# All four granules of the last two pairs split instead of two split and two in fp32

## What is computed

```
mod = jax.nn.silu(c) @ w_mod + b_mod
shift, scale, gate = jnp.split(mod, 3, axis=-1)
h = rms_norm(x, g_pre) * (1.0 + scale[:, None, :]) + shift[:, None, :]
proj = h @ w_in
```

## Time and profile before

| | us |
|---|---|
| median of 3 runs (2849.79 to 2851.85) | 2849.89 |
| the profiled execution's own time | 2849.23 |
| its span | 2847.5 |

### The profile page before, as it was taken

How to read it: one execution, slowest core, us unless ns; L and a number is a source line. 1 busy time by engine, 2 the same in 40 slices (tenths; PEclk the granted TensorE clock), 3 DMA queues, 4 the chain that set the end, 5 groups by cost and what they waited for, 6 DMA issues and landing times.

```text
span 2847.5 us, 35784 instructions
## 1 busy us (share of the span) xinstructions
PE 2803.5 (98%) x13342; PEld 2302.4 (81%) x13342; DVE 1767.3 (62%) x2180; ACT 1382.0 (49%) x1879; POOL 36.2 (1%) x69
## 2 busy tenths in 40 slices
PE   8899999999999999999999999999999999999998
PEld 5588887888887888888888888788888888888886
DVE  7789899777656556554544556675555545445565
ACT  3355646456544454544554544445444445545443
POOL 0000000000000000000000000000000000000000
PEclk8999999999999999999999999999999999999999
DMA  9987798865655555565555566555555655555664
GB/s 398 409 306 236 280 344 306 287 221 179 206 177 183 170 171 178 175 222 192 171 178 177 174 196 223 178 178 170 173 177 190 206 192 170 178 177 176 196 213 148
DMA packets 159991, 603.73 MB, mean 212 GB/s; under 512 B 18376, under 2 KB 18576, under 8 KB 154464
## 3 DMA queue, kind: packets, MB, share of 16 engines
q1 hardware_dynamic: 155376, 583.08, 59.8%
q0 software_dynamic: 4464, 18.55, 2.0%
HBM read 599.41 MB, written 2.14 MB: 211 GB/s over the span
## 4 chain that ended last, share of the span: by engine, by line
PE 93%; DVE 3%; DMA 3%; ACT 1%; issue 0%; SPq 0%; ACTq 0%; DVEq 0%
PE acc L785 63%; PE acc L2334 19%; DMA raw<-in_w 3%; PE psT L733 2%; PE psS L766 1%; PE psS L756 1%; PE psS L2334 1%; PE psT L2247 1%; PE psS L2300 1%; PE psT L2260 1%; PE psT L739 1%; PE psS L2319 0%; PE psT L2225 0%; DVE wlo L1771 0%; PE psS L2272 0%; PE psS L773 0%
## 5 line engine op out<-in xcount | busy, mean ns | idle before, releaser
L434 DVE TENSOR_TENSOR wlo<-raw,whi 128x1024 fp32r<-128x1024 f32 x670 | 820.3, 1225 | 868.0 <-ACT whi L322 866.6
L322 ACT ACTIVATE whi<-raw 128x1024 fp32r<-128x1024 f32 x670 | 709.2, 1059 | 996.0 <-PE acc L785 974.9
L785 PE MATMUL acc<-whi,tokens_hi 128*128 128x512 f32 x2304 | 637.4, 398 | 3.5 <-DVE tokens_lo L279 1.9
L785 PE MATMUL acc<-whi,tokens_lo 128*128 128x512 f32 x2304 | 619.1, 390 | 0.0
L785 PE MATMUL acc<-wlo,tokens_hi 128*128 128x512 f32 x2304 | 618.9, 390 | 0.0
L785 PEld LDWEIGHTS acc<-whi,tokens_lo 128*128 128x128 f32 x2304 | 432.8, 188 | 92.2
L785 PEld LDWEIGHTS acc<-wlo,tokens_hi 128*128 128x128 f32 x2304 | 432.8, 188 | 91.5
L785 PEld LDWEIGHTS acc<-whi,tokens_hi 128*128 128x128 f32 x2304 | 422.5, 188 | 84.0 <-DVE tokens_lo L440 2.2
L1771 DVE TENSOR_TENSOR wlo<-raw,whi 128x1024 fp32r<-128x1024 f32 x160 | 195.4, 1223 | 99.3 <-ACT whi L1468 98.8
L1468 ACT ACTIVATE whi<-raw 128x1024 fp32r<-128x1024 f32 x160 | 168.7, 1058 | 181.4 <-PE acc L2334 117.0
L2334 PE MATMUL acc<-whi,tokens_hi 128*128 128x512 f32 x800 | 225.5, 402 | 1.9 <-DVE tokens_lo L1870 1.2
(11 more groups left out here) (353 smaller groups left out, 2268.8 us busy)
## 6 DMA issues: line engine op xcount, KB each, us to landing
raw<-in_w SPq DMA_DIRECT2D x838, 512.0 KB, 3.4
raw<-in_w_late SPq DMA_DIRECT2D x80, 512.0 KB, 5.0
mraw<-in_w SPq DMA_DIRECT2D x64, 512.0 KB, 4.7
mraw<-in_w_late SPq DMA_DIRECT2D x48, 512.0 KB, 4.8
y<-in_w_early SPq DMA_DIRECT2D x12, 1024.0 KB, 14.2
mraw<-in_w_early SPq DMA_DIRECT2D x7, 1024.0 KB, 13.8
scr<-in_w_early SPq DMA_DIRECT2D x7, 1024.0 KB, 13.5
sgl<-in_w_early SPq DMA_DIRECT2D x6, 1024.0 KB, 14.6
```

Of the source, the lines that this page charges most:

```text
L322: act.activation(whi[:, n % SLOTS, :], raw[:, n % SLOTS, :], ACT.Copy).then_inc(s_hi, 1)
L434: dve.tensor_tensor(wlo[:, n % SLOTS, :], raw[:, n % SLOTS, :], whi[:, n % SLOTS, :].bitcast(F32), ALU.subtract).then_inc(s_lo, 1)
L785: m = pe.matmul(acc[c % 2][:, tb, :], a[:, kk, tb * P:(tb + 1) * P], b[:, n % SLOTS, k * CW:(k + 1) * CW], start=(kk == 0 and q == 0), sto ...
```

## The change

`direct` now holds for granules below `R_SPLIT` (24) instead of 32. So in pairs 6 and 7 the granules 24, 25, 28 and 29 are split as well. They use slots 0 and 1 of `raw`, `whi` and `wlo`; the transfer of granule 28 waits for the `lo` of 24 and that of 29 for the `lo` of 25, and those of granule 32 and of the first `w_late` tile wait for the `lo` of 28 and 29. ACT gets four `hi` more, DVE four `lo`, PE 48 split matmuls for 16 in fp32. ACT's `fill_hi` of pairs 6 and 7 is moved from the first step of the pair to its third. PE's first granule of these pairs waits for `tokens_lo` instead of `zt`.

```diff
--- before.py
+++ after.py
@@ -959,7 +959,7 @@
 
 def direct(n):
 
-    return n < R_RING and n % TOGETHER[0] < DIRECT
+    return n < R_SPLIT and n % TOGETHER[0] < DIRECT
 
 
 def splits(n):
@@ -970,6 +970,21 @@
 def landing(n):
 
     return divmod(DIRECT * (n // TOGETHER[0]) + n % TOGETHER[0], LANDINGS)
+
+
+def place_of(n):
+
+    return landing(n)[1] if direct(n) else n % SLOTS
+
+
+def turns_before(i, n):
+
+    return sum(not direct(m) for m in range(i, n, SLOTS))
+
+
+def last_in(i, n):
+
+    return max(m for m in range(n) if place_of(m) == i)
 
 
 def done(l, c):
@@ -984,6 +999,7 @@
 R_RING = TOGETHER[0] * GPC
 DIRECT = 2
 LANDINGS = 3 * DIRECT
+R_SPLIT = TOGETHER[0] * (GPC - 2)
 R_FULL = (63, 64, 70, 99, 100, 107, 115, 119)
 RING = SLOTS + 2
 CLOSE1 = 2
@@ -1038,8 +1054,8 @@
 
 
     if item in ITEM:
-        return ITEM[item] // RING + 1 + (R_RING // SLOTS if DIRECT <= ITEM[item] % RING < SLOTS else 0)
-    return item[1] // SLOTS + 1
+        return ITEM[item] // RING + 1 + (turns_before(ITEM[item] % RING, R_RING) if ITEM[item] % RING < SLOTS else 0)
+    return turns_before(item[1] % SLOTS, item[1] + 1)
 
 
 def h_fill(l, r):
@@ -1376,7 +1392,7 @@
                 sp.dma_start(whole(n), dram["w1"][n]).then_inc(s_d[landing(n)[1]], 16)
                 return
             if n >= SLOTS:
-                sp.wait_ge(*split(n - SLOTS))
+                sp.wait_ge(*released(last_in(n % SLOTS, n)))
             sp.dma_start(slot(("w", n)), dram["w1"][n]).then_inc(s_w[n % SLOTS], 16)
 
         def item(k):
@@ -1385,7 +1401,7 @@
             if k >= RING:
                 sp.wait_ge(*consumed(ITEMS[k - RING]))
             elif k < SLOTS:
-                sp.wait_ge(*released(max(n for n in range(R_RING) if (landing(n)[1] if direct(n) else n % SLOTS) == k)))
+                sp.wait_ge(*released(last_in(k, R_RING)))
             else:
                 sp.wait_ge(s_macc, EARLY - (EARLY - 1) % len(big))
             src = dram["w1"][i] if kind == "w" else dram["w_late"][i]
@@ -1589,7 +1605,7 @@
                     fill_hi(("h", l, h_fill(l, r)))
                 if r == GRAN1 - 1:
                     act.activation(one[:], eps[:, 0:1], ACT.Sqrt)
-                if l == 0 and r in range(TOGETHER[0], R_RING, TOGETHER[0]):
+                if l == 0 and r in list(range(TOGETHER[0], R_SPLIT, TOGETHER[0])) + list(range(R_SPLIT + 2, R_RING, TOGETHER[0])):
                     fill_hi(("h", l, r // TOGETHER[0]))
                 if not direct(GRAN1 * l + r) and (l == 0 or r >= AHEAD):
                     hi(GRAN1 * l + r)
@@ -2406,9 +2422,9 @@
                 continue
             c, g = place(l, r)
             if l == 0 and r < R_RING:
-                if c == 0:
+                if direct(r) and c == 0:
                     pe.wait_ge(s_aff, g + 1)
-                if c == DIRECT:
+                if c == (DIRECT if direct(r - c) else 0):
                     pe.wait_ge(s_h, g + 1)
             elif c == 0:
                 pe.wait_ge(s_h, GPC * l + g + 1)
```

## The result

| | before | changed |
|---|---|---|
| median, us | 2850.52 (2849.78 to 2851.91, 6 runs) | 2873.89 (2870.49 to 2875.87, 6 runs) |
| ratio to before | | 1.0083 [1.0073, 1.0092] |
| span of the profiled execution | 2847.5 | 2868.8 |

What follows compares the result with a forecast made beforehand. It took transfers to bound the opening and PE, without gaps, the long rest. Terms +2.0 (tile 29), +1.3 (tokens_lo), -1.6 (fp32 matmuls gone), +0.8 (hole) make +2.5, forecast 2852.4 us, range 2849.4 to 2857.0.

Steps and rivals of the forecast that it cites:

- The early pairs: Pairs ahead of pair 6: claimed untouched by the change, with no term in the sum.
- Pair 6 on ACT and DVE: Later tokens_hi and a third lo start DVE's tile 29 at 126.2 to 126.5 instead of 124.16; taken as +2.0.
- The hand-over and PE in pair 7: PE starts pair 7 on tokens_lo instead of zt, +1.3; four split granules take 10.9 instead of 12.44, -1.6.
- The clock in pair 6: PE, idle 7.3 before pair 6, then runs slow and loses 1.7; bounds 0 to +0.9 on pair 7's start, taken 0.
- the cover: Room for a slow clock: PE ends pair 6 at 133.7 at full clock, and its next start is 135.8.
- The hole: Wait at 147.84 before the small product, behind the emptied queue and ACT's hi of granule 35: longer by +0.8.
- my upper bound: Latest landing of granule 35's transfer, 149.5, with the small product then starting at 151.8, +3.2.
- my +1.8 at granule 32: PE starts granule 32 at 146.7 instead of 144.96, after its four split granules of pair 7.
- (a): Rival: DVE absorbs the added lo, so the fp32 saving shows; -0.2, or -3.1 if pair 6 counts too; chance 0.12.
- (b): Rival: PE's clock stays low through all of pair 6, pair 7 starts 8.8 later; +10.6, 2860.5; chance 0.08.
- (c): Rival: emptied queue costs more, granule 32's or 35's transfer later than the bound; with 3 more 2855.9; chance 0.12.

Runs made afterwards that it cites:

- e1_places: Changed kernel with place_of giving a direct granule a slot number only where it lands in raw; 2856.34 us, ratio 1.0023.
- e2_waits: Kernel before with only the transfers of granules 6, 7, 18 and 19 waiting for the matmuls of 4, 5, 16 and 17; 2868.25 us, ratio 1.0063.
- e3_first: Kernel before with only the transfers of granules 6 and 7 waiting for the matmuls of 4 and 5; 2859.71 us, ratio 1.0031.
- e6_pair7: e1_places with R_SPLIT at 28, so only pair 7 has four split granules; 2853.13 us, ratio 1.001.
- e5_copies: e1_places with ACT's copies of chunks 2 and 3 moved right behind the hi of granule 33; 2850.92 us, ratio 1.0002.
- e7_pair7_copies: e6_pair7 with the copies of chunks 2 and 3 moved as in e5_copies; 2850.19 us, ratio 1.0.
- e4_second: Kernel before with only the transfers of granules 18 and 19 waiting for the matmuls of 16 and 17; 2858.97 us, ratio 1.003.

## Why the prediction was wrong

**The early pairs.** The step that failed is the sentence "The early pairs are untouched". I had read the diff of `weights`, `last_in(n % SLOTS, n)` for `n - SLOTS`, as another way to say the same wait, and compared the orders of ACT and DVE around pair 6 and SP's only from there on. It put at nothing a term of +17.3 to +18.0 (change less e1_places; e2_waits), most of the error of 21.5; the rest is the hole below. It was no rival either. What the profile of before could have told: these waits stand at the head of the one queue for all large transfers, the DMA share is 1.00, and a wait there that outlasts the transfers in hand is not made good (e3_first).

**Pair 6 on ACT and DVE, +2.0.** Right: 126.14 in e1_places, and e6_pair7, which leaves pair 6 alone, has `zt` of pair 7 at 131.43 and tile 29 at 124.22.

**The hand-over and PE in pair 7, +1.3 and -1.6.** Right in size: pair 7 at 135.90, granule 32 at 146.94, 2.0 late instead of 1.8.

**The clock in pair 6.** PE stood idle 7.32 before it and then needed 4.39 for its first granule (122.88 to 127.27), 1.7 more than the 2.72 of a split one. That is the 1.7 that I put behind the cover, and the start of pair 7 waited only 0.28 for `tokens_lo`: the cover was just long enough, as taken. The 1.7 is no fixed price: the same granule lost 1.8 in the changed kernel (idle 6.44) and 2.4 in e5_copies (idle 8.38).

**The hole, +0.8.** The mechanism was right (an emptied queue, a late transfer, ACT's copy behind a `hi`), the size was not. Measured are +3.0 for the hole and +1.6 for the clock behind it, 4.6 in all, against the 0.8 of my sum. My issue times for the refilled queue were right to 0.1 (134.6, 137, 138.1, 139.3; measured 134.49, 137.01, 138.14, 139.28). What failed is that I let granule 35's transfer follow the others at full rate, from 135 on, to land between 148.0 and 149.5. It stood behind one more wait, for the `lo` of granule 32, whose own landing was late by the same hole; it was issued at 144.24 and landed at about 151.3, 1.8 beyond my upper bound. I also read ACT as if it waited for this landing alone. The earlier trace rows show no idle time before the `hi` of granule 35: already before, its landing and the end of ACT's work behind the `hi` of granule 34 fell together, and that path came 5.1 later too. And I priced idle time of PE as idle time only, without the slower clock behind it. Put right, the sum without the early pairs is +6.6 at granule 33, and the median of e1_places says +6.0. That my +1.8 at granule 32 came out nearly exactly was no help to the total, since what followed it was off by 3.8.

**The rivals.** (a), the saving that comes through, is false for this change by its own mark: tile 29 started at 126.14, not by 124.36. Where its condition holds, in e7_pair7_copies (`zt` of pair 7 at 131.50, and the hole closed), the ratio is 1.0, so its -0.2 is neither shown nor refuted; PE's 1.4 less in pair 7 only repays its later start on `tokens_lo`. Its -3.1 for both pairs lies outside the interval of e5_copies (at best -2.0), which splits both and closes the hole. (b), the slow clock through pair 6, is false: it was back by about 127. (c), a dearer emptied queue, is right in kind for the part of the change that was described: granule 35 did land 1.8 later than my bound, and its 2855.9 (by its own terms rather 2856.1) is 5.4 above the median of before, where e1_places is 6.0 above. But 1.6 of the 6.0 is the clock, which (c) did not have. None of the three holds for the whole.

## What to carry to other kernels

Where a change rewrites a wait, compare the full order of that queue with the semaphores it waits for, from its first row, and not only where the change is meant; two counters that both run from 0 but number different memories are the place to look. A wait at the head of the only transfer queue costs nothing while the transfers in hand last (some 13 and 16 us here) and at least its rest after that, and here, with the DMA engines as the bound, two such losses added up. An instruction that only frees a buffer (the copies here) is safer ahead of one that waits for a transfer in the same engine's order: it took the 6.0 back here, though in the kernel before it gained nothing that could be measured.

## What the runs showed of the hardware

After idle times of about the same length PE's clock sometimes fell and sometimes not. Before the small product PE stood idle 3.76 in e1_places, and the granted clock went from 1.00 to 0.50; it stood idle 3.14 in the changed kernel, and the clock fell as well (7.31 for the product instead of 5.69); it stood idle 3.06 in e6_pair7, and the clock stayed at 1.00:

```profile
151.00:152.00 1.00, 1.00 (x10) 0.81 (x10) 0.97 (x5) 0.87 (x1) 0.00 (x0) 1.00 1.04 426
```

So an idle time of 3 us cost 1.6 us more in one kernel than in another. The section HAM oscillation of "TensorE: Matmul & The Clock Gate" in the Trainium skill says that waits for DMA can put PE back to its lower clock again and again; the first two traces agree with it, the third is a wait of nearly the same length without it.

Other idle times of PE in these traces say more plainly that length alone does not decide. The clock fell after idle times of 1.82 (e2_waits, before granule 4: 5.40 instead of 3.70) and 2.2 (before pair 6 in the kernel before: 8.83 for 16 records, where after 1.51 in e7_pair7_copies they took 7.13). It did not fall after 2.83 (e4_second) and 2.99 (e2_waits) before pair 7, where 8 records took 3.70.
